# Value units of a sparse-attention decode branch: groups of five in every other slot instead of two or three in each

## What is computed

```python
q, kc, vc, ks, vs, kw, vw, g, z = jnp.split(xn @ prm['w_in_c'][li], split_points(C_SIZES), axis=-1)
...
o_cmp, o_sel = compressed_and_selected(q, q_rot, pos, k_cmp, v_cmp, n_past + S, fetch)
o_win = band_attention(q_rot, kw_all, vw_all, w_off, C_WIN)
gate = jax.nn.sigmoid(g.astype(jnp.float32)).reshape(B, S, 3, C_KV_HEADS, C_GQA, 1)
o = gate[:, :, 0] * o_cmp + gate[:, :, 1] * o_sel + gate[:, :, 2] * o_win
y = (o.reshape(B, S, C_WIDTH).astype(h.dtype) * jax.nn.silu(z)) @ prm['w_out_c'][li]
```

## Time and profile before

| | |
|---|---|
| three runs | 1813.58, 1813.9, 1820.62 us, median 1813.9 us |
| profiled execution | 1816.0 us, of which the span of instructions is 1814.3 us |
| busy share of the span | PE 95%, PEld 88%, DVE 60%, ACT 45%, POOL 10% |
| granted TensorE clock, mean | 0.987 |
| stage of the change | 64 slots between about 1362 and 1598 us |

### The profile page before, as it was taken

How to read it: one execution, slowest core, us unless ns; L and a number is a source line. 1 busy time by engine, 2 the same in 40 slices (tenths; PEclk the granted TensorE clock), 3 DMA queues, 4 the chain that set the end, 5 groups by cost and what they waited for, 6 DMA issues and landing times.

```text
span 1814.3 us, 43768 instructions
## 1 busy us (share of the span) xinstructions
PE 1732.4 (95%) x17501; PEld 1593.7 (88%) x17501; DVE 1079.5 (60%) x1847; ACT 820.9 (45%) x1715; POOL 188.7 (10%) x360
## 2 busy tenths in 40 slices
PE   6999999988999989989988999999999999989999
PEld 5899999888888879979977998888988888889998
DVE  4478888777644454434566898654455444465464
ACT  4344444444334333334456554444355545444544
POOL 3000000000000000000000002333232433300000
PEclk9999999999999979999999999999999999999999
DMA  7888888653588647867655556787777878755454
GB/s 238 307 279 275 271 276 278 226 149 117 187 261 279 228 141 255 291 245 233 199 186 163 143 160 211 252 265 247 222 237 225 279 251 280 254 188 180 165 179 139
DMA packets 287096, 406.49 MB, mean 224 GB/s; under 512 B 18640, under 2 KB 223087, under 8 KB 285880
## 3 DMA queue, kind: packets, MB, share of 16 engines
q1 hardware_dynamic: 260196, 320.00, 54.9%
q0 software_dynamic: 26624, 83.92, 14.4%
q10 hardware_dynamic: 92, 0.02, 0.0%
HBM read 391.43 MB, written 12.45 MB: 223 GB/s over the span
## 4 chain that ended last, share of the span: by engine, by line
PE 76%; DVE 16%; ACT 3%; issue 2%; DMA 2%; SPq 0%; ACTq 0%; DVEq 0%
PE PJ L1716 47%; PE XB L2123 4%; PE XB L1742 4%; DVE w_low L1070 3%; PE XB L2135 2%; PE XB L2209 2%; DVE proj L1089 2%; PE XB L2190 2%; PE XB L2014 1%; DVE scr L1089 1%; PE XB L1856 1%; PE XB L2165 1%; ACT w_up L656 1%; PE XB L1759 1%; PE XB L1816 1%
## 5 line engine op out<-in xcount | busy, mean ns | idle before, releaser
L1716 PE MATMUL PJ<-xh,w_up 128*128 128x264 f32 x3072 | 918.6, 299 | 30.3 <-DVE xl L1113 15.7
L1716 PE MATMUL PJ<-xl,w_up 128*128 128x264 f32 x3072 | 876.9, 285 | 0.0
L1716 PE MATMUL PJ<-xh,w_low 128*128 128x264 f32 x3072 | 875.8, 285 | 0.0
L1070 DVE TENSOR_TENSOR w_low<-wring,w_up 128x512 fp32r<-128x512 f32 x768 | 523.8, 690 | 428.9 <-ACT w_up L656 419.2
L656 ACT CAST w_up<-wring 128x512 fp32r<-128x512 f32 x768 | 472.4, 619 | 427.9 <-PE PJ L1716 336.3
L1716 PEld LDWEIGHTS PJ<-xh,w_up 128*128 128x128 f32 x3072 | 583.8, 190 | 56.0 <-DVE w_low L1070 17.2
L1716 PEld LDWEIGHTS PJ<-xl,w_up 128*128 128x128 f32 x3072 | 583.6, 190 | 2.0
L1716 PEld LDWEIGHTS PJ<-xh,w_low 128*128 128x128 f32 x3072 | 581.3, 189 | 0.0
L624 POOL DMA_DIRECT2D cring<-in_cache_c_sel_kv_dram x256 | 137.8, 538 | 1351.6 <-issue 1056.3
L917 ACT COPY kcmp<-XB 128x512 f32<-128x512 f32 x80 | 46.9, 586 | 136.6 <-PE XB L2123 136.5
L1418 DVE COPY kcmp<-XB 128x512 f32<-128x512 f32 x80 | 55.3, 692 | 81.2 <-PE XB L2123 79.9
(11 more groups left out here) (326 smaller groups left out, 1519.6 us busy)
## 6 DMA issues: line engine op xcount, KB each, us to landing
wring<-in_w_in_ab_dram SPq DMA_DIRECT2D x144, 512.0 KB, 4.8
cring<-in_cache_c_cmp_kv_dram SPq DMA_DIRECT2D x128, 512.0 KB, 5.2
cring<-in_cache_c_sel_kv_dram POOLq DMA_DIRECT2D x256, 256.0 KB, 3.9
wring<-in_w_in_c_dram SPq DMA_DIRECT2D x112, 512.0 KB, 4.3
wring<-in_w_ple_gate_dram SPq DMA_DIRECT2D x64, 512.0 KB, 4.5
cring<-in_cache_a_kv_dram SPq DMA_DIRECT2D x48, 512.0 KB, 5.1
wring<-in_w_out_ab_dram SPq DMA_DIRECT2D x32, 512.0 KB, 6.0
cring<-in_cache_c_win_kv_dram POOLq DMA_DIRECT2D x64, 256.0 KB, 4.6
```

The costliest lines, as they stand in the source:

```text
L1070: nc.vector.tensor_tensor(w_low[:, e % NE], raw(e), w_up[:, e % NE].bitcast(F32), ALU.subtract).then_inc(sem("w_lo"), 1)
L1716: ins = nc.tensor.matmul(PJ[(2 * bl + c) % 4][:, 0:T], w[:, e % NE, k, tileT(c)], x[:, kx, :], start=(kx == 0 and w is w_up and x is xh), ...
```

## The change

`VU` becomes 32 groups of five units, in slots 5 + 57n/31 rounded down: 5, 6, 8, 10, 12, 14, 16, 17, 19, ... 62. Two neighbouring groups stand two slots apart 26 times and one slot apart five times (5 and 6, 16 and 17, 27 and 28, 38 and 39, 49 and 50). A sample has four groups. Nothing else is edited; the slots of `out_T`, `take_out` and `add_new` follow from `VU`. The file is 7 lines shorter above them, so that line 2209 reads 2202 after the change, and so on.

```diff
-        VU = {}
-        t_ = 5
-        for b_ in range(B):
-            parts = (3, 3, 3, 3, 2, 2, 2, 2) if b_ in (2, 5) else (3, 3, 3, 3, 3, 3, 2)
-            for n_, size in enumerate(parts):
-                VU[t_] = list(range(20 * b_ + sum(parts[:n_]), 20 * b_ + sum(parts[:n_ + 1])))
-                t_ += 1
-        assert t_ == 63
+        VU = {5 + n * 57 // 31: list(range(5 * n, 5 * n + 5)) for n in range(32)}
```

## The result

The change is slower: 1830.4 us at the median of five runs (1827.3 to 1832.4) against 1817.05 us for five runs of the kernel before, ratio 1.0075, 95% interval 1.0054 to 1.0095. Run a second time, beside other kernels, it stood at 1827.6 us against 1817.15, ratio 1.0053 (1.0034 to 1.0071). The forecast was +10.6 us; the two measurements are +13.3 and +10.5 us. In absolute terms it was 1824.5 us in a range of 1816 to 1832, and 1830.4 lies near the upper end; 3.2 of the 5.9 us between them come from the kernel before, which stands at 1817.05 with five runs and stood at 1813.9 with three.

A forecast was written before the change was run, and what follows sets the result against it. PE was taken to set the pace in the second half of the odd layer's projection. Terms -4.2 + 9.8 + 2.5 + 0.8 + 1.7 = +10.6 us on 1813.9 gave 1824.5 us, range 1816 to 1832.

The forecast's parts named there:

- 26 groups fewer: Odd layer's projection, second half: 58 groups of value units become 32, each saving 0.16 us of PE time, -4.2 us.
- five one-slot pairs: Slots 6, 17, 28, 39, 50: PE waits for the fifth unit's page, as the ring is not refilled, +9.8 us.
- two-slot distances: Other 26 group distances: 13 are ties between the fifth unit's landing and its use, 0.2 us mean wait each, +2.5 us.
- heads: Prompt heads: slots without values expose waits on DVE, 0.15 us in slots 18, 22, 26, 37, more in 33; net +0.8 us.
- clock: After the long ring waits: one drop to half clock for 3.40 us, +1.7 us, with none and three drops as bounds.
- What bounds it: Second half of the odd layer's projection: PE sets the pace, busy 227.22 of 236.00 us, and never waits behind a value unit.
- The ring refills faster: Rival, value units' DMAs: landings 1.3 us shorter, five waits total 3.5 us, ties vanish; +0.1 us, 1814.0 us; chance 0.17.
- Bursts meet the weights: Rival, DMA queues: five units and a weight quarter queue together, landings take 0.5 us more; 1831 us; chance 0.18.
- The heads bind everywhere: Rival, 26 bare slots: DVE and ACT need the values as cover, about 0.5 us each, 13 us; about 1832; chance 0.05.

The follow-up runs named there:

- the ring of twelve: The change with twelve places in the ring for the value units instead of eight; ratio 0.9981 to the kernel before, stage 3.6 us shorter.

## Why the prediction was right, point by point

With the ring of twelve as the change without waits, the stage's +11.9 us of the first profile divides as follows; the waits are summed from the gaps inside the groups, and the clock is what slots 17, 18, 50 and 51 took beyond the ring of twelve and beyond their waits.

| term | predicted | measured |
|---|---|---|
| 26 groups fewer | -4.2 | -4.0 |
| five one-slot pairs | +9.8 | +8.1 |
| two-slot distances | +2.5 | +2.5 |
| heads | +0.8 | +0.4 |
| clock | +1.7 | +5.0 |

- **What bounds it.** It held that PE sets the pace and that the cover of the ring was made for three units: the largest new waits are behind the value pages, inside the groups, before the fourth and fifth unit.
- **Groups.** 0.155 us against 0.16, and the 0.21 us step into a head's values stays.
- **One-slot pairs.** The five waits were put at 1.06, 2.33, 1.91, 1.46 and 2.99 us; slots 6, 17, 28, 39 and 50 show about 0.2, 2.3, 1.0, 1.6 and 2.9. Three are within 0.2 us; slots 6 and 28 came out 0.9 us short, since the page of their fifth unit landed within 3.3 us, where the median of 4.1 was put in. For slot 28 the timelines of POOL and PE show the issue, 2.84 us behind the group's start at 1465.85 as summed, and the unit taken 3.27 us later:

```profile
1468.69 0.54 POOL L617 DMA_DIRECT2D cring<-in_cache_c_sel_kv_dram  x1 [0.62 <-issue]
```

```profile
1471.96 0.43 PE L2202 MATMUL XB<-cring,kcmp 128*32 128x128 f32 x8 [0.49 <-DMA cring<-in_cache_c_sel_kv_dram]
```

  POOL's pace of 1.16 us for a page with a number is half of the mechanism: reads taken out of the way removed 5.5 of 11.6 us of waiting.
- **Two-slot distances.** 2.5 us in sum, but not 13 small ties: five waits in slots 8, 16, 43, 45 and 60, of 0.1 to 1.0 us. The second profile has 2.4 us, in part in other slots (25 and 62 instead of 16 and 43). With the pairs spread, the weight loads' waits in all such places came to 1.7 us.
- **Heads.** Slot 33 waits 1.3 us instead of 0.8, and slot 52 takes its two units for nothing, as foreseen. Of the four slots put at 0.15 us each, 22 and 37 lose 0.2 us with the ring of twelve (their heads start 0.40 and 0.43 us after the last projection matmul, against 0.21 elsewhere); 18 and 26 show no wait, since the transposes of a finished sum (`out_T`) stand there after the change, which the sum had overlooked.
- **Clock: the term that was mis-sized.** "I count one drop, 1.7 us" took its price from one stretch of 3.40 us. The first profile had two, of 3.4 and 10.2 us, worth about 1.5 and 3.6 us; the second had one of 6.8 us, worth about 2.5. A us at half clock cost 0.35 to 0.44 us, near the half that was put in; the number and the length of the stretches were what was off. The bound of three drops, 5.1 us, held it. That the sum came so near to the stage's +11.9 is in part luck: the clock was put 3.3 us too low, and the one-slot pairs 1.7 us too high.
- **Rivals.** "The ring refills faster" needed landings below 3.4 us: the median stayed at 4.1, 2.8 being the fastest. The pages of slots 6 and 28, within 3.3 us, are two of the five that did land as it had it. By the Trainium skill (DMA: Bandwidth & Descriptors, Anatomy of one DMA) the estimate was 2.6 us; no row of before or of the change supports it in this stage. "Bursts meet the weights" foretold nearly the measured time, but by landings 0.5 us slower, and they were not slower: a right number by a wrong way. At the median, landings grew clearly only where POOL's issues were closer still, to 4.6 us. "The heads bind everywhere" falls with the ring of twelve, whose 26 bare slots cost 0.4 us together.

## What to carry to other kernels

Before work is gathered into larger lots, compare the time from a buffer's release to its being full again (here 1.7 us to the issue, 1.16 us for each place further, 4 to 5 us to land) with the shortest distance between two lots, not with the mean: five pairs out of 31 distances made nearly all the loss; with these pairs spread the gathering came out even (0.9994), and with four more places it gained (0.9981). Price a new wait on TensorE of the length seen here, 1.6 us and more, higher than its length, since the half clock that came with such waits cost 1.5 to 3.6 us more in the two profiles of the change. And a lot of work that must go somewhere is free where the engine waits for another: moving four groups into such waits gained 3.3 us, the whole gathering 3.6.

## What was not expected of the hardware

- The half clock behind a wait has no fixed length. Single ring waits of 1.57, 1.79, 1.90, 2.17, 2.33 and 2.52 us in this stage each came with it, for about 3.4, 6.8, 10.2, 6.8, 10.2 and 13.6 us (twice the windows' shortfall from 1.00); ring waits of up to 1.34 us in the same stage did not. Longer waits mostly had longer stretches, the one of 2.17 us being an exception. One wait that no kernel of this study changes shows the spread best. Right behind the stage PE waits 4.04 us for DVE, where no ring is in play, and half clock came with it in all twelve profiles, for 3.4 us in seven and 6.8 us in five. Before:

```profile
1598.60 0.59 PE L1716 MATMUL PJ<-xh,w_up 128*128 128x264 f32 x1 [4.04 <-DVE xl L1113]
```

```profile
1598.60:1601.60 3.00, 3.00 (x13) 3.00 (x14) 3.00 (x3) 1.08 (x1) 0.00 (x0) 0.50 0.98 418
```

- In slots 50 and 51 the half clock cost more than the wait that it followed (3.6 against 2.9 us): heads, values and projection are all slower in it. That the clock follows from the idle time itself, and not from what else comes with the pair, is argued from these six places in five profiles, and from the wait of 4.04 us on another engine, and not shown by a run that changes the idle time alone.
- Five DMAs of 256 KB in a group did not land later than two or three did (4.1 us at the median, before 4.3), with pages that need a number issued 1.16 us apart; with the numbers read ahead (seven issues in 4.17 us) it was 4.6.
